# Reading the moving columns and writing the output columns of the main matmuls from last to first

## The chip, the cores and the metric

The kernel runs on one core of one Trainium2 chip. The metric is the device time of that core in microseconds (us). Three executions of the kernel before took 2253.87, 2256.15 and 2256.82 us; the median is 2256.15 us.

## The reference

One inference step of a two-layer decoder trunk (the constant DEPTH is 2) over a prompt of 256 tokens and 8 single-token samples, which share all weights. Everything is float32, D_MODEL is 2048.

```
for i in range(DEPTH):                                    # DEPTH = 2
    hp, hs = rmsnorm(xp, g_mix_pre[i]), rmsnorm(xs, g_mix_pre[i])
    if i % 2 == 0:   # w_in 2048 x 4608, window attention + gated width-3 convolution, w_out 2048 x 2048
        op, osm = even_prompt(hp, ...), even_sample(hs, ...)
    else:            # w_in 2048 x 4096, gelu, layernorm, 128 x 128 position mixing, w_out 2048 x 2048
        op, osm = cmlp_prompt(hp, ...), cmlp_sample(hs, ...)
    xp, xs = xp + rmsnorm(op, g_mix_post[i]), xs + rmsnorm(osm, g_mix_post[i])
    # ffn(h) = square(relu(h @ w_up)) @ w_down, hidden width 8192
    xp = xp + rmsnorm(ffn(rmsnorm(xp, g_ffn_pre[i]), w_ffn_up[i], w_ffn_down[i]), g_ffn_post[i])
    xs = xs + rmsnorm(ffn(rmsnorm(xs, g_ffn_pre[i]), w_ffn_up[i], w_ffn_down[i]), g_ffn_post[i])
```

It returns the two activations and the new windows and states of both groups. Nearly all arithmetic is in the dense products `h @ w`.

## The kernel before

The activations lie with channels on the 128 partitions and tokens in the free dimension: a tile such as `hhi` is 128 x 16 x 264, 16 channel tiles of 264 columns (T = 256 prompt tokens and 8 samples). The tokens of one channel tile are neighbours in memory, 4 bytes apart, so a product reads them in one run.

Every dense product goes in blocks of 256 output channels (BC). A block's weights are 2048 x 256 values. SyncE loads them in two halves of 1 MB into `raw` (four slots, so two blocks ahead). ScalarE writes their rounded high part `whi` (L586), VectorE the remainder `wlo` (L952), in quarters of four channel tiles. The activations are kept in the same manner as `hhi` and `hlo` (or `ahi` and `alo`). The high and the low parts have the type float32r.

TensorE's work on a block is `quarter` (L1342 and after), called four times. For each of the four channel tiles k of a quarter and each of the two output tiles j, three matmuls add into one PSUM region of 264 columns: `whi` with `hi` (L1353), `whi` with `lo` (L1354) and `wlo` with `hi` (L1355). So a block has 16 x 2 x 3 = 96 such matmuls. Each has its own weight load of 128 columns (called PEld in the profile) and streams 264 moving columns. These are the "main matmuls": 17088 of them in 178 blocks. The block number's parity picks one of two pairs of PSUM banks (0 and 1, or 2 and 3), and VectorE or another reader takes the finished pair out (for instance L1188, L1214) while the next block runs. Readers always wait for the whole block (`w_used`, raised by the last matmul of a quarter).

Beside them TensorE does small work in banks 4 to 7: transposes, attention, the position mixing (L1704), and the statistics of the norms. `statistic` (L1370, L1374) multiplies a constant 128 x 128 matrix with 264 columns of plain float32; `token_statistic` (L1381) multiplies with one column. Each plain float32 matmul stands in the trace as two.

The order on each engine is the order in which the code is written; waits on semaphores tie the engines together. Names that matter below: `ps` is PSUM, `out` is the PSUM region of a main matmul, `hi` and `lo` are its moving tiles, `L979` writes `hlo` after a norm.

Of the kernel before, what the change touches and what calls it, by code (L numbers as in the profile page):

```python
# [33 lines left out]
CH = D // P  # L34
# [3 lines left out]
T = SEQ + NB  # L38
# [46 lines left out]
def build(nc, io):  # L85
    ctx = ExitStack()
    with ctx:
        def sb(name, shape, dt=F32):
            return ctx.enter_context(nc.sbuf_tensor(name, shape, dt))
# [6 lines left out]
        whi = sb("whi", [P, CH, BC], F32R)  # L96
        wlo = sb("wlo", [P, CH, BC], F32R)
# [95 lines left out]
        ps = ctx.enter_context(nc.psum_tensor("ps", [P, 8, 512], F32))  # L193
# [1147 lines left out]
        def _(pe):  # L1341
            def quarter(n, par, q, hi, lo, operand=None):  # L1342

                if q == 0 and not (isinstance(n, int) and n < 2):
                    pe.wait_ge(taken, n - 1)
                pe.wait_ge(w_lo_ready, 4 * n + q + 1)
                for k in range(QK * q, QK * q + QK):
                    if operand:
                        operand(k)
                    for j in range(2):  # L1350
                        cols = slice(P * j, P * j + P)
                        out = ps[:, 2 * par + j, 0:T]
                        pe.matmul(out, whi[:, k, cols], hi[:, k, :], start=(k == 0), stop=False)  # L1353
                        pe.matmul(out, whi[:, k, cols], lo[:, k, :], start=False, stop=False)  # L1354
                        mm = pe.matmul(out, wlo[:, k, cols], hi[:, k, :], start=False, stop=(k == CH - 1))  # L1355
                mm.then_inc(w_used, 1)

            def h_operand(k_norm):
# [52 lines left out]
            for q in range(NQ):  # L1411
                if q == NQ - 1:

                    pe.wait_ge(state_in, 16)
                    pe.wait_ge(l_in, 16 * 3)
                    pe.wait_ge(x_ready, PAIRS)
                    n_small = 2 * CH + 3 * CONVT
                    pe.transpose(ps[:, 7, 0:n_small], g_rows[0:n_small, 1, :], ident[0:n_small, 0:n_small])
                    for c in range(CONVT):
                        mm = pe.transpose(ps[:, 4, 16 * c:16 * c + 16], state_tok[0:2 * NB, P * c:P * c + P],  # L1420
                                          ident[0:2 * NB, 0:2 * NB])
                    mm.then_inc(state_turned, 1)
                quarter(0, 0, q, hhi, hlo, h_operand(0))
                for c in {0: (5, 6), 1: (7,)}.get(q, ()):
                    turn_x(c)
# [126 lines left out]
            for n in range(1, N_EOUT):  # L1552
                for q in range(NQ):
                    quarter(n, n % 2, q, hhi, hlo)
                    even_task(n, q)
# [13 lines left out]
            def product(n0, hi, lo, operand, pairs=UNIT // 2):  # L1569
                with pe.Fori(0, pairs) as i:  # L1570
                    for par in range(2):
                        for q in range(NQ):
                            quarter(n0 + 2 * i + par, par, q, hi, lo, operand if par == 0 else None)
# [11 lines left out]
            for c in range(CONVT):  # L1585
                mm = pe.transpose(ps[0:2 + NB, 4 + c // 4, P * (c % 4):P * (c % 4) + P], z_last[:, c, :], ident[:, :])
# [178 lines left out]
```

## Time and profile before

| What | Before |
|---|---|
| three executions, us | 2253.87, 2256.15, 2256.82 |
| profiled execution: time, us | 2253.87 |
| its span, first to last instruction, us | 2253.9 |
| TensorE busy | 2204.5 us, 98% |
| VectorE busy | 1249.2 us, 55% |
| ScalarE busy | 996.3 us, 44% |
| GpSimd busy | 237.5 us, 11% |
| bytes moved by DMA | 386.72 MB, mean 172 GB/s |
| main matmuls | 17088 of 17771 matmuls in the trace |

How to read it: the profiled execution is the shortest of the three, and nothing lies around its span, so its time is its span. Matmuls overlap in the array. The duration of one (about 0.29 us) is therefore longer than the distance from one start to the next, and it is this distance, here called the pitch, that adds up to the span. A pitch is read either from the starts in the timeline or from a count of matmuls over a stretch in which TensorE has no gap.

### The profile page before, as it was taken

The page shows a single profiled execution, that of the slowest core. Times are in us where ns is not written, and L with a number is a line of the kernel's source. Part 1 is how long each engine was busy: PE and PEld are TensorE (multiplying, and loading weights), DVE is VectorE, ACT ScalarE, POOL GpSimd, SP SyncE. Part 2 cuts the span into 40 slices and gives each one's busy share as a digit, 9 for nine tenths or more (in the row PEclk, how much of TensorE's full clock was granted, in tenths as well). Part 3 has the DMA queues.
Part 4 walks back from the last instruction along what each step waited for, and adds up shares of the span by engine and source line. Part 5 has one row for each costly group of instructions (what it writes and reads, how often), then busy time and mean ns, then how long its engine had stood idle before and what let it go on. Part 6 is the DMA issues. An engine that isn't in the chain of part 4 may idle for free.

```text
span 2253.9 us, 43497 instructions
## 1 busy us (share of the span) xinstructions
PE 2204.5 (98%) x17771; PEld 2183.2 (97%) x17771; DVE 1249.2 (55%) x1318; ACT 996.3 (44%) x1243; POOL 237.5 (11%) x178
## 2 busy tenths in 40 slices
PE   7999998999999999999989999989999999999999
PEld 7999997999999999999979999989999999999998
DVE  7556756654554455455576675575445545545543
ACT  5544444443443344344444564444334434434443
POOL 3001213000000000011241201220000000001112
PEclk9999999999999999999999999989999999999999
DMA  6854453555655655555535455545555555555551
GB/s 215 229 172 133 155 178 112 187 178 176 186 171 184 212 179 182 173 185 169 185 112 185 155 168 181 172 130 170 185 175 178 182 173 184 172 182 179 174 177 68
DMA packets 380631, 386.72 MB, mean 172 GB/s; under 512 B 6805, under 2 KB 378317, under 8 KB 380431
## 3 DMA queue, kind: packets, MB, share of 16 engines
q1 hardware_dynamic: 374530, 380.02, 53.8%
q10 hardware_dynamic: 6036, 5.80, 0.8%
q8 instruction: 45, 0.74, 0.1%
q14 instruction: 20, 0.16, 0.0%
HBM read 380.10 MB, written 5.71 MB: 171 GB/s over the span
## 4 chain that ended last, share of the span: by engine, by line
PE 93%; DVE 5%; ACT 1%; DMA 0%; issue 0%; POOL 0%; DVEq 0%; SPq 0%; ACTq 0%
PE ps L1353 30%; PE ps L1354 30%; PE ps L1355 30%; DVE hlo L979 2%; DVE wlo L952 1%; DVE y L1001 1%; PE ps L1635 0%; PE ps L1704 0%; PE ps L1548 0%; DMA region<-in_x_prompt_dram 0%; PE ps L1534 0%; PE ps L1467 0%; DVE region L1336 0%; DVE y L1006 0%; DVE x L1007 0%; DVE rs_post L971 0%
## 5 line engine op out<-in xcount | busy, mean ns | idle before, releaser
L952 DVE TENSOR_TENSOR wlo<-raw,whi 128x1024 fp32r<-128x1024 f32 x712 | 894.5, 1259 | 823.1 <-ACT whi L586 822.8
L586 ACT ACTIVATE whi<-raw 128x1024 fp32r<-128x1024 f32 x712 | 753.1, 1060 | 1092.9 <-PE ps L1355 1088.7
L1353 PE MATMUL ps<-hhi,whi 128*128 128x264 f32 x3136 | 906.2, 289 | 32.8 <-DVE hlo L979 32.5
L1354 PE MATMUL ps<-hlo,whi 128*128 128x264 f32 x3136 | 900.1, 287 | 0.0
L1355 PE MATMUL ps<-hhi,wlo 128*128 128x264 f32 x3136 | 898.5, 287 | 0.0
L1354 PE MATMUL ps<-alo,whi 128*128 128x264 f32 x2560 | 730.4, 285 | 0.0
L1353 PE MATMUL ps<-ahi,whi 128*128 128x264 f32 x2560 | 729.3, 285 | 0.0
L1355 PE MATMUL ps<-ahi,wlo 128*128 128x264 f32 x2560 | 729.0, 285 | 0.0
L1353 PEld LDWEIGHTS ps<-hhi,whi 128*128 128x128 f32 x3136 | 598.5, 191 | 43.1 <-issue 29.5
L1355 PEld LDWEIGHTS ps<-hhi,wlo 128*128 128x128 f32 x3136 | 596.7, 190 | 0.0
L1354 PEld LDWEIGHTS ps<-hlo,whi 128*128 128x128 f32 x3136 | 596.6, 190 | 0.1
L1353 PEld LDWEIGHTS ps<-ahi,whi 128*128 128x128 f32 x2560 | 483.5, 189 | 0.4 <-issue 0.4
L1355 PEld LDWEIGHTS ps<-ahi,wlo 128*128 128x128 f32 x2560 | 482.1, 188 | 0.0
L1354 PEld LDWEIGHTS ps<-alo,whi 128*128 128x128 f32 x2560 | 481.5, 188 | 0.0
L464 POOL COPY acc_pre<-sq 128x528 f32<-128x528 f32 x5 | 4.3, 870 | 762.8 <-ACT sq L816 741.8
L1188 DVE TENSOR_TENSOR y<-y,ps 128x528 f32 (+2 forms) x66 | 45.2, 687 | 60.7 <-PE ps L1355 60.7
L467 POOL TENSOR_TENSOR acc_pre<-acc_pre,sq 128x528 f32<-128x528 f32 x35 | 56.8, 1623 | 156.7 <-ACT sq L816 140.5
L1214 DVE TENSOR_SCALAR region<-ps 128x528 f32<-128x528 f32 x64 | 45.2, 707 | 39.1 <-PE ps L1355 39.1
L467 POOL TENSOR_TENSOR acc_post<-acc_post,sq 128x528 f32<-128x528 f32 x24 | 41.4, 1725 | 224.2 <-ACT sq L606 224.2
L979 DVE SCALAR_TENSOR_TENSOR hlo<-x,gains,hhi 128x264 fp32r<-128x264 f32 x64 | 50.2, 824 | 1.0 <-ACT hhi L614 1.0
L614 ACT ACTIVATE hhi<-x,gains 128x264 fp32r<-128x264 f32 x64 | 29.5, 507 | 41.2 <-POOL x L490 26.2
L1217 DVE TENSOR_TENSOR alo<-region,ahi 128x528 f32 x64 | 45.3, 708 | 0.5 <-ACT ahi L822 0.5
(218 smaller groups left out, 763.2 us busy)
## 6 DMA issues: line engine op xcount, KB each, us to landing
raw<-in_w_ffn_up_dram SPq DMA_DIRECT2D x128, 1024.0 KB, 5.3
raw<-in_w_ffn_down_dram SPq DMA_DIRECT2D x128, 1024.0 KB, 5.5
raw<-in_w_in_even_dram SPq DMA_DIRECT2D x36, 1024.0 KB, 5.2
raw<-in_w_in_cmlp_dram SPq DMA_DIRECT2D x32, 1024.0 KB, 5.3
raw<-in_w_out_even_dram SPq DMA_DIRECT2D x16, 1024.0 KB, 5.5
raw<-in_w_out_cmlp_dram SPq DMA_DIRECT2D x16, 1024.0 KB, 5.5
region<-in_x_prompt_dram SPq DMA_DIRECT2D x4, 512.0 KB, 8.5
out_y_prompt_dram<-region SPq DMA_DIRECT2D x8, 256.0 KB
```

What stands on the lines that cost most here:

```text
L467: pool.tensor_tensor(acc[:, :, :], acc[:, :, :], sq[:, s % 2], ALU.add).then_inc(sq_used, 1)
L586: act.activation(whi[:, QK * q:QK * q + QK, :], raw[:, 2 * par + q // 2, k, :], ACT.Copy).then_inc(w_hi_ready, 1)
L614: ins = act.activation(hhi[:, t, :], x[:, t, :], ACT.Copy, scale=gains[:, G_PRE[k], t:t + 1])
L952: dve.tensor_tensor(wlo[:, QK * q:QK * q + QK, :], raw[:, 2 * par + q // 2, k, :], whi[:, QK * q:QK * q + QK, :].bitcast(F32), ALU.subtrac ...
L979: ins = dve.scalar_tensor_tensor(out=hlo[:, t, :], in0=x[:, t, :], scalar=gains[:, G_PRE[k], t:t + 1], in1=hhi[:, t, :].bitcast(F32), op0= ...
L1001: dve.tensor_tensor(y[:, 2 * c:2 * c + 2, :], y[:, 2 * c:2 * c + 2, :], twice(rs_post[:, :]), ALU.mult).then_inc(scaled, 1)
L1188: return dve.tensor_tensor(dst, dst, src, ALU.add) if add else dve.tensor_copy(dst, src)
L1214: dve.tensor_scalar(relu[:, :, :], pair(par), 0.0, None, ALU.max).then_inc(taken, 1)
L1217: dve.tensor_tensor(alo[:, bass.ds(4 * i + 2 * par, 2), :], asq[:, :, :], ahi[:, bass.ds(4 * i + 2 * par, 2), :].bitcast(F32), ALU.subtrac ...
L1353: pe.matmul(out, whi[:, k, cols], hi[:, k, :], start=(k == 0), stop=False)
L1354: pe.matmul(out, whi[:, k, cols], lo[:, k, :], start=False, stop=False)
L1355: mm = pe.matmul(out, wlo[:, k, cols], hi[:, k, :], start=False, stop=(k == CH - 1))
```

## The change

In `quarter` the slice of the moving operand and the slice of the output are both taken with a step of -1 along the 264 columns. Column 263 is read first and its result is written to column 263, and so on down to column 0. The value that lands in each PSUM column is the same sum as before. The weights are read as before; no other matmul, wait, tile or loop is touched. Each engine has the same instructions in the same order as before. In the built program the moving pattern of such a matmul goes from step 1, offset 0 to step -1, offset 263, and so does the output's.

```
-                        out = ps[:, 2 * par + j, 0:T]
-                        pe.matmul(out, whi[:, k, cols], hi[:, k, :], start=(k == 0), stop=False)
-                        pe.matmul(out, whi[:, k, cols], lo[:, k, :], start=False, stop=False)
-                        mm = pe.matmul(out, wlo[:, k, cols], hi[:, k, :], start=False, stop=(k == CH - 1))
+                        out = ps[:, 2 * par + j, 0:T][:, ::-1]
+                        pe.matmul(out, whi[:, k, cols], hi[:, k, ::-1], start=(k == 0), stop=False)
+                        pe.matmul(out, whi[:, k, cols], lo[:, k, ::-1], start=False, stop=False)
+                        mm = pe.matmul(out, wlo[:, k, cols], hi[:, k, ::-1], start=False, stop=(k == CH - 1))
```

## Rows read from the trace of the kernel before

**Rows 1.** The page, busy time of each engine: us, share of the span, instructions.
```profile
PE 2204.5 (98%) x17771; PEld 2183.2 (97%) x17771; DVE 1249.2 (55%) x1318; ACT 996.3 (44%) x1243; POOL 237.5 (11%) x178
```

**Rows 2.** The page, busy tenths in 40 slices, with the granted clock.
```profile
PE   7999998999999999999989999989999999999999
...
PEclk9999999999999999999999999989999999999999
```

**Rows 3.** The page, the chain that ended last: shares by engine.
```profile
PE 93%; DVE 5%; ACT 1%; DMA 0%; issue 0%; POOL 0%; DVEq 0%; SPq 0%; ACTq 0%
```

**Rows 4.** The page, the main matmuls: count, busy us, mean ns, idle before, releaser.
```profile
L1353 PE MATMUL ps<-hhi,whi 128*128 128x264 f32 x3136 | 906.2, 289 | 32.8 <-DVE hlo L979 32.5
L1354 PE MATMUL ps<-hlo,whi 128*128 128x264 f32 x3136 | 900.1, 287 | 0.0
L1355 PE MATMUL ps<-hhi,wlo 128*128 128x264 f32 x3136 | 898.5, 287 | 0.0
L1354 PE MATMUL ps<-alo,whi 128*128 128x264 f32 x2560 | 730.4, 285 | 0.0
L1353 PE MATMUL ps<-ahi,whi 128*128 128x264 f32 x2560 | 729.3, 285 | 0.0
L1355 PE MATMUL ps<-ahi,wlo 128*128 128x264 f32 x2560 | 729.0, 285 | 0.0
```

**Rows 5.** Windows: us, busy us and count of each engine, clock, DMA share, GB/s.
```profile
600.00:1000.00 400.00, 400.00 (x3267) 400.00 (x3266) 203.13 (x189) 165.70 (x177) 9.64 (x5) 1.00 0.59 184
1500.00:2100.00 600.00, 600.00 (x4900) 600.00 (x4900) 304.43 (x282) 248.28 (x264) 8.46 (x5) 1.00 0.57 178
386.56:388.70 2.14, 2.14 (x12) 2.14 (x11) 2.14 (x4) 0.58 (x3) 1.49 (x1) 0.50 0.00 0
```

**Rows 6.** Timeline of TensorE at 386 us: start us, us, engine, line, operation.
```profile
386.39 0.42 PE L1354 MATMUL ps<-hlo,whi 128*128 128x264 f32 x1
386.61 0.42 PE L1355 MATMUL ps<-hhi,wlo 128*128 128x264 f32 x1
386.83 0.42 PE L1353 MATMUL ps<-hhi,whi 128*128 128x264 f32 x1
```

**Rows 7.** Timeline of TensorE at 1184 us.
```profile
1184.01 0.28 PE L1354 MATMUL ps<-hlo,whi 128*128 128x264 f32 x1
1184.12 0.28 PE L1355 MATMUL ps<-hhi,wlo 128*128 128x264 f32 x1
1184.24 1.05 PE L1370 MATMUL ps<-acc_pre,mean_w 128*128 128x264 f32 x4
1185.16 0.39 PE L1353 MATMUL ps<-hhi,whi 128*128 128x264 f32 x1
```

**Rows 8.** Timeline of TensorE at 2137 us.
```profile
2137.44 1.39 PE L1381 MATMUL ps<-mean_w,acc_pre 128*128 128x1 f32 x12
2138.69 0.37 PE L1353 MATMUL ps<-ahi,whi 128*128 128x264 f32 x1
```

**Rows 9.** Groups of PE by line: a plain 264-column group, one column, 16 apart.
```profile
L1370 PE MATMUL ps<-acc_pre,mean_w 128*128 128x264 f32 x16 | 4.2, 386 | 0.0
...
L1381 PE MATMUL ps<-mean_w,acc_pre 128*128 128x1 f32 x12 | 1.4, 243 | 0.0
...
L1601 PE MATMUL ps<-region,mean_w 1*128 1x16 f32 x2 | 0.4, 268 | 0.0
```

**Rows 10.** Waits of PE: us in total, times, longest us.
```profile
PE ps L1353 <- DVE hlo L979: 32.5, 20, 8.0
```

## The prediction

> **What bounds the kernel.** I read the busy line first, then the slices, then the chain, then the groups of TensorE, and last the distance from start to start. TensorE is busy 98% of the span, VectorE 55%, ScalarE 44% [rows 1]. The slices show that this is no average over unlike stages: TensorE stands at 9 in nearly every slice, at full granted clock [rows 2]. The chain that ended last runs 93% over TensorE [rows 3]. Six groups hold the main matmuls, 3 x 3136 + 3 x 2560 = 17088, with no idle time before them but 32.8 us at L1353 [rows 4], nearly all of it waits for `hlo` after a norm [rows 10]. So what counts is the pitch of a main matmul.
>
> A duration of 285 to 289 ns [rows 4] is not the pitch, because matmuls overlap. Two long stretches in which TensorE has no gap give it: 400 us over 3267 is 122.4 ns, 600 us over 4900 is 122.4 ns [rows 5]. That is the same number in two different halves of the kernel, with VectorE and ScalarE at about half load in both. In all: 17088 x 122.45 = 2092 us of the 2253.9 us span. The other 162 us are small matmuls, the waits, the start and the end. The profiled execution's time is its span; the median of the three runs is 2.3 us above it.
>
> **The change, part by part.** No instruction, wait or DMA is added, removed or moved. The three matmuls of `quarter` keep 264 columns, the same bytes, the same bank and the same weight load. Two things differ in each of the 17088: the addresses on the moving side descend, and so do those on the PSUM side. So the sum has one line: 17088 x (new pitch - 122.45 ns). Each nanosecond of pitch is 17.1 us. Nothing hides it: with TensorE without a gap for hundreds of us, every extra nanosecond of pitch is on the path. Nor can another engine take a gain away soon, since VectorE is at 203 of 400 us there and the DMAs at 0.59 [rows 5].
>
> Nothing else follows from the order within a matmul. Readers of PSUM wait for a whole quarter, not for its first column, so it does not matter to them which column is written last. In three matmuls in a row that add into the same region each column comes up again one pitch later, before as after, because all three are turned. At the step from one region to the next (and from a small matmul to a main one) the order is free anyway. The waits of 32.5 us end with VectorE's `hlo` [rows 10], which the change does not touch.
>
> No row of this kernel has a descending run, so the two new costs have to be bounded. I take them together, since one pitch shows both.
>
> From above. At half clock the pitch of the same matmul is 220 ns [rows 6] (12 starts in 2.14 us at clock 0.50 [rows 5]), which is 264 columns at one per 1.2 GHz tick. At full clock the plain float32 matmul of the same 264 columns has a pitch of (1.05 us - 0.386 us) / 3 = 221 ns [rows 7, 9]. So if the array got only one column per 1.2 GHz tick from the descending run, or could write only one, the pitch would be 220 to 222 ns: 17088 x 99.5 = +1700 us. A middle value comes from the only row that reads columns far from each other, L1601 with 16 columns 512 bytes apart: 268 ns against 243 ns for one column [rows 9], 25 ns for 15 more columns, 1.7 ns each, where L1370 has 221 / 264 = 0.84 ns. That form is another (one row of the array, plain float32) and the two durations are of two and twelve records, so I hold it for weak; it says only that a price between nothing and double is possible.
>
> From below. The stream itself needs no more than half the pitch at half clock, 220 / 2 = 110 ns, and 122.4 are paid. If what fills these 12.4 ns had to do with ascending order, the pitch could fall to 110: 17088 x -12.4 = -212 us. A one-column matmul with the same weight load has a pitch of about (1.39 - 0.24) / 11 = 0.104 us [rows 8, 9], so the weight load alone costs nearly as much as the stream. The 12.4 ns may thus come from the weight side. In that case a descending stream that is up to 12 ns dearer would cost nothing either.
>
> The value that I take is zero. The two ends, -212 and +1700 us, lie far apart and the row nearest to the changed matmul is the matmul itself: same type, same count, same bytes, neighbours still neighbours, the run still in one piece and its even length still splitting into aligned pairs. The two rows at the upper end are nearest in what would have to happen, not in what is changed. Sum: 2253.9 + 0, and 2256 us against the median.
>
> The Trainium skill says on its page Advanced Engine Details and Errata, section Memory Cachelines, that SBUF delivers at full rate as long as a 16-byte line is hit at least twice in a row. A descending float32 run hits each line four times, so by this rule the moving side costs nothing; no row before can confirm it. The same section, and PSUM — Partial Sum Buffer in its Specifications table, speak against the change: PSUM lines have 8 bytes, "any non-contiguous AP slows matmuls significantly". The page does not say whether a step of -1 is contiguous. Taken strictly it makes the output side pay, and the sum would be the one with the upper end; taken by pairs in a line, 263 with 262, it costs nothing. VectorE's page of the microarchitecture (Vector Engine (DVE) Microarchitecture Reference, section 5.1) counts steps of +1 and of -1 alike for its paired modes; that is another engine, and I use it only to lean.
>
> **The rivals.**
> 1. The pair is lost: two neighbouring columns are served in one 1.2 GHz tick only when they ascend, on the moving or the output side. For: at full clock 264 columns go by in 122.4 ns, 1.8 per tick of 1.2 GHz, so whatever feeds the array and takes its results works at twice that tick or in pairs. Against: the pairs stay aligned. Pitch 222 ns, time 2254 - 2092 + 17088 x 0.222 = 3955 us. The stretches at half clock would not change, at 220 ns already. The strict reading of the skill's PSUM rule above is this case.
> 2. A partial price: a cost per line or per instruction of a descending run, from above 12 ns on if the weight side covers the first, otherwise from 0. The middle row's ratio, 1.7 / 0.84 = 2.0 put on 122.4 ns, would reach past the upper bound, so it sets no place between the ends. 5 ns are +85 us, 2341 us against the median; half way, 172 ns, is +847 us, 3103 us.
> 3. The other side, faster: the 12.4 ns above the stream come from the moving run and the weight run both ascending, and starting on the same side of their tiles, and a descending stream passes the weight reads with less waiting. From 110 ns: 2254 - 212 = 2042 us, between them in proportion, decided as soon as the pitch drops by 0.3 ns (5 us). For: the 12.4 ns are unexplained, and plain float32 pays for its 264 columns in two streams only 221 ns, 110.5 each. Against: the pitch is equal in stretches with unlike load and with different tiles, which looks like a fixed cost per matmul.
> 4. The change doesn't do what it says: since both sides are turned together, something between the code and the engine may turn both back. Its time is that of no change, 2256 us, and its chance is part of my forecast's; an experiment with one side alone would be needed to tell.
>
> **How the numbers follow.** No change in pitch (with 4): 0.59. Pair lost: 0.20. Partial price: 0.14. Faster: 0.07. 0.2% is 4.5 us, a pitch of 0.26 ns, and about what a measurement of this kernel can tell from nothing. So faster 0.07, same 0.59, slower 0.34. The likeliest case alone would be 2251 to 2261 us. It leaves 0.41 outside; the range therefore reaches over the partial price to the pair lost, 3955 us and a little for the start, and down to 2240 for a small gain. That leaves out 0.06.
>
> **What would show it.** Right: in the windows at 600 to 1000 and 1500 to 2100 us again 3267 and 4900 matmuls, durations of the six groups at 285 to 289 ns, steps of 0.12 us in the timeline, waits for `hlo` at 32.5 us, the statistic's pitch at 0.22. Rival 1: steps of 0.22 us at granted clock 1.00, about 1800 matmuls in 400 us, VectorE's share down to a third. Rival 2: a pitch between. Rival 3: more than 3267. My forecast is wrong if the pitch moves by 0.3 ns either way while the clock row stays as it is; if the pitch stands and the time moves, I have overlooked a wait.

## The result and the profile after

The changed kernel took 2229.61 us (median of 4 runs, 2228.98 to 2229.94), the kernel before 2255.86 us in the same comparison (4 runs). The ratio is 0.9885, with a 95% interval of 0.9873 to 0.9897: the change makes the kernel 1.15% faster, 26 us. The prediction had no change as likeliest, and the lower end of its range was 2240 us.

The page of the changed kernel, busy line, slices and chain:

```profile
PE 2176.4 (98%) x17771; PEld 2154.9 (97%) x17771; DVE 1249.9 (56%) x1318; ACT 995.6 (45%) x1243; POOL 236.9 (11%) x178
...
PE   7999998999999999999989999989999999999999
...
PEclk9999998999999999999999999989999999999999
...
PE 92%; DVE 6%; ACT 1%; DMA 0%; issue 0%; DVEq 0%; SPq 0%; ACTq 0%
```

TensorE is as full as before [rows 1 to 3], over a span of 2227.3 us, 26.6 us shorter. (The execution behind this trace took 2228.98 us, 1.7 us more than its span, and so it is in every later run. The span of 2253.9 us of the kernel before therefore belongs more likely to its execution of 2255.57 us than to the one of 2253.87 us; that its time is its span was a wrong reading, by under 2 us.) VectorE, ScalarE and GpSimd work as long as before, to within 1 us. Nothing has left the path; what stands on it has become shorter.

The groups of the main matmuls, after (columns as in rows 4), and the waits for `hlo` (as in rows 10):

```profile
L1353 PE MATMUL ps<-hhi,whi 128*128 128x264 f32 x3136 | 902.6, 288 | 33.4 <-DVE hlo L979 33.1
L1354 PE MATMUL ps<-hlo,whi 128*128 128x264 f32 x3136 | 895.4, 286 | 0.0
...
L1353 PE MATMUL ps<-ahi,whi 128*128 128x264 f32 x2560 | 727.0, 284 | 0.0
```

```profile
PE ps L1353 <- DVE hlo L979: 33.1, 20, 8.0
```

The durations fell by 1 to 2 ns, the waits stayed [rows 4, 10]. The end of a matmul is modelled in the trace, so the pitch is read from counts. Windows of the changed kernel, columns as in rows 5:

```profile
600.00:1000.00 400.00, 400.00 (x3313) 400.00 (x3312) 205.53 (x190) 168.18 (x180) 11.41 (x6) 1.00 0.59 186
1500.00:2100.00 600.00, 600.00 (x4968) 600.00 (x4967) 308.40 (x286) 252.00 (x268) 12.08 (x7) 1.00 0.58 181
```

3313 matmuls instead of 3267 in 400 us, 4968 instead of 4900 in 600 us [rows 5]: the pitch is 120.8 ns and was 122.4. Over all neighbouring main matmuls at full clock the mean distance of starts went from 122.44 to 120.88 ns (steps of 200 ns and more, which hold a wait, left out). The some 16,800 such steps make 26.3 us, nearly the whole of the 26.6 us. At half clock the step is 220 ns in both kernels.

Looking closer than a window gives the cause away. The starts in one block of the kernel before, the channel tile k = 3, and in the changed kernel, tiles k = 1 and k = 2 (start us, us, engine, line):

```profile
708.92 0.29 PE L1353 MATMUL ps<-ahi,whi 128*128 128x264 f32 x1
709.05 0.28 PE L1354 MATMUL ps<-alo,whi 128*128 128x264 f32 x1
709.17 0.29 PE L1355 MATMUL ps<-ahi,wlo 128*128 128x264 f32 x1
709.30 0.29 PE L1353 MATMUL ps<-ahi,whi 128*128 128x264 f32 x1
...
709.68 0.28 PE L1353 MATMUL ps<-ahi,whi 128*128 128x264 f32 x1
```

```profile
710.76 0.28 PE L1353 MATMUL ps<-ahi,whi 128*128 128x264 f32 x1
710.88 0.28 PE L1354 MATMUL ps<-alo,whi 128*128 128x264 f32 x1
711.00 0.28 PE L1355 MATMUL ps<-ahi,wlo 128*128 128x264 f32 x1
...
711.48 0.28 PE L1353 MATMUL ps<-ahi,whi 128*128 128x264 f32 x1
...
712.22 0.28 PE L1353 MATMUL ps<-ahi,whi 128*128 128x264 f32 x1
```

Six matmuls take 0.76 us at k = 3 before (709.68 - 708.92), 0.72 us at k = 1 after and 0.74 us at k = 2 after. The pitch is not one number, it hangs on the channel tile. Averaged over all blocks from 550 to 1040 us and from 1500 to 2130 us, by the matmul's place in its block (worked out from the starts in the two traces, ns):

```
k (same again for k + 8)      0      1      2      3      4      5      6      7   mean
before                     119.9  121.9  121.3  125.4  123.8  122.1  124.9  120.8  122.5
changed                    120.2  120.3  123.1  122.4  120.4  120.1  120.1  120.1  120.8
```

The pattern repeats after eight channel tiles, in both kernels, to 0.1 ns. Neighbouring moving tiles start 1056 bytes apart, and 8 x 1056 = 33 x 256. The weight tiles start 1024 = 4 x 256 bytes apart. So the place of the moving run against the weights' run comes back after eight tiles, in units of 256 bytes. Four of the eight tiles of the changed kernel (k = 0 and 5 to 7) stand at a flat 120.0 ns, with 0.8 ns more at the first of the six matmuls; only k = 2 and 3 are over 121 ns.

### The profile page after: what moved, and what is told of

The parts are those of the page before. It is cut to its first block, busy times and chain, and to the rows that moved or that the text cites. A ratio compares the mean times of both kernels' runs of the same rounds, so it can differ in the third digit from the quotient of the medians.

```text
span 2227.3 us, 43497 instructions
## 1 busy us (share of the span) xinstructions
PE 2176.4 (98%) x17771; PEld 2154.9 (97%) x17771; DVE 1249.9 (56%) x1318; ACT 995.6 (45%) x1243; POOL 236.9 (11%) x178
## 4 chain that ended last, share of the span: by engine, by line
PE 92%; DVE 6%; ACT 1%; DMA 0%; issue 0%; DVEq 0%; SPq 0%; ACTq 0%
PE ps L1353 30%; PE ps L1355 30%; PE ps L1354 30%; DVE hlo L979 2%; DVE wlo L952 1%; DVE y L1001 1%; ACT whi L586 0%; PE ps L1635 0%; DMA region<-in_x_prompt_dram 0%; PE ps L1704 0%; PE ps L1548 0%; PE ps L1534 0%; PE ps L1467 0%; DVE region L1336 0%; DVE y L1006 0%; DVE x L1007 0%
```

## The experiments

Theory A: TensorE reads the moving columns of one matmul while it loads the weights of the next. Both are reads of SBUF, they get in each other's way, and how often depends on where the two runs stand and which way they go. Theory B: the writing side does it. That loading and streaming go on at the same time is to be seen in the kernel before, where the weight load of each matmul (PEld) begins with the matmul ahead of it:

```profile
600.05 0.29 PE L1355 MATMUL ps<-hhi,wlo 128*128 128x264 f32 x1
600.05 0.20 PEld L1353 LDWEIGHTS ps<-hhi,whi 128*128 128x128 f32 x1
600.18 0.29 PE L1353 MATMUL ps<-hhi,whi 128*128 128x264 f32 x1
600.18 0.19 PEld L1354 LDWEIGHTS ps<-hlo,whi 128*128 128x128 f32 x1
```

All pitches below are means over the same two stretches as in the table, each from the one execution of a kernel that was traced; the times beside them are medians of all its executions. All times of the kernel before are medians from the same chip as the kernel they stand beside.

**One side at a time.**

```
 e1:  out = ps[:, 2 * par + j, 0:T]              pe.matmul(out, whi[:, k, cols], hi[:, k, ::-1], ...)   (lo the same)
 e2:  out = ps[:, 2 * par + j, 0:T][:, ::-1]     pe.matmul(out, whi[:, k, cols], hi[:, k, :], ...)      (lo the same)
```

> Only the moving columns are read from last to first; the output columns are written first to last (so the products' columns come out mirrored). Theory A (the 1.6 ns of pitch come from the reading side: moving read and weight read get in each other's way less when the moving run descends): pitch 120.8 ns as in the changed kernel, time about 2230 us, and the same pattern over the 48 matmuls of eight channel tiles. Theory B (it is the writing side, the order in which PSUM columns are written): pitch 122.5 ns, 2256 us. Theory C (both sides must be turned together, only their agreement matters): neither, at least as slow as before.

> Only the output columns are written from last to first; the moving columns are read first to last (columns come out mirrored). Theory A: pitch 122.5 ns, 2256 us, pattern as before the change. Theory B: 120.8 ns, 2230 us. Theory C: neither.

Moving side alone: 2229.22 us (4 runs), ratio 0.9886 (0.9869 to 0.9902), pitch 120.8 ns, and the same eight pitches as the changed kernel to 0.1 ns. Output side alone: 2256.25 us (10 runs), ratio 1.0002 (0.9992 to 1.0011), pitch 122.5 ns and the eight of the kernel before. Windows of e1 and of e2:

```profile
600.00:1000.00 400.00, 400.00 (x3312) 400.00 (x3312) 205.88 (x191) 167.97 (x181) 11.44 (x6) 1.00 0.60 186
```

```profile
600.00:1000.00 400.00, 400.00 (x3268) 400.00 (x3267) 203.15 (x189) 165.88 (x178) 9.63 (x5) 1.00 0.59 184
```

So the gain comes whole from reading in descending order. Writing PSUM in descending order costs and gives nothing. Theories B and C are out, and so is the fourth rival (that the change doesn't do what it says).

**Is it the tile that is read, or the place in the program?**

```
-  hi[:, k, :]                   lo[:, k, :]
+  hi[:, 4 * par + q, :]         lo[:, 4 * par + q, :]            (e3)
+  hi[:, 4 * par + q, ::-1]      lo[:, 4 * par + q, ::-1]         (e4, output turned too)
```

> Ascending as before the change, but all 24 matmuls of a quarter stream one channel tile, number 4 x parity + quarter, so tiles 0 to 7, instead of tile k (the products are other ones). The tiles start 1056 bytes apart, that is 32 bytes further each in units of 256 bytes. Theory A (what counts is where the moving tile starts against the weights' run): the pitch is constant within a quarter after its first matmuls and differs by tile, over a spread of about 4 to 6 ns between the best and the worst tile (by the means of the run before: tiles 0 and 7 about 120 to 121, tiles 3, 4 and 6 about 124 to 125). Theory D (the pattern over 48 matmuls comes from the place of the instructions in the program, not from the addresses): the pattern over k stays as before whatever tile is read.

> Turned, and one channel tile per quarter (number 4 x parity + quarter) as in the ascending one before. Theory A': the quarters on tiles 2 and 3 have pitches of 122 to 124 ns, the six others 120.0; mean about 120.6 to 120.9. Rival (descending reads simply cost less everywhere, and the tile change costs): all eight at 120.0.

```
tile                           0      1      2      3      4      5      6      7
e3, ascending                121.4  121.9  121.0  121.8  123.3  121.7  120.6  120.0
e4, turned                   120.0  120.0  124.4  122.2  120.0  120.0  120.0  120.0
```

(Means after the first channel tile of each quarter; e3 took 2243.44 us in one run, e4 2228.93.) With one tile read throughout a quarter the pattern over k goes and the pitch is the tile's own. Theory D falls. In e4 two tiles are dear, the same two as in the changed kernel, and six stand at 120.0 flat. The rival that descending reads are cheaper everywhere fails on tiles 2 and 3. In e3 the values by tile are not those I had expected: tiles 3, 6 and 4 were the dear ones in the kernel before, and of these only tile 4 is here. The pitch at a place depends on what went before it, so a number from one arrangement doesn't carry over to another.

**Is the weight load the other party?** First a case in which it reads almost nothing of SBUF: one weight column, 128 times over.

```
-  pe.matmul(out, whi[:, k, cols], ...)
+  pe.matmul(out, whi[:, k, P * j:P * j + 1].to_broadcast([P, P]), ...)       (wlo the same)
```

> Ascending as before the change, but the weight load reads one column 128 times over instead of 128 columns (all 128 output channels of a tile come out alike), so the weight side reads a single spot of SBUF while the moving side reads as before. Theory A (the two reads collide): the pattern over the eight tiles goes or becomes quite another one; if a fixed spot is hit seldom, the pitch is near the floor of 120 ns. Rival (the moving read alone has the pattern, or writes of other engines): pattern and 122.5 ns stay as before.

Windows of e7, with ascending reads:

```profile
600.00:1000.00 400.00, 400.00 (x3332) 400.00 (x3331) 207.82 (x193) 170.35 (x183) 11.35 (x6) 1.00 0.60 186
1500.00:2100.00 600.00, 600.00 (x4997) 600.00 (x4996) 311.03 (x288) 255.22 (x273) 13.96 (x8) 1.00 0.58 182
```

120.1 ns for every one of the eight tiles, 2219.03 us in one run. (Within a tile the single steps still go from 116.7 to 122.5 ns; their mean is what is flat. The weight load takes 189 ns in the trace, before 190, so it isn't a shorter load that shows here.) The moving reads and their order are those of the kernel before, and VectorE, ScalarE and the DMAs write as before. So the extra above 120 ns is not the moving read's own and not a matter of the other engines: it needs a weight load that walks over its 512 bytes.

**Tiles that all stand alike.** The weight tiles are put 1056 bytes apart, like the moving tiles, so the relation is the same for every k; e6 is turned as well.

```
-  whi = sb("whi", [P, CH, BC], F32R)         +  whi = sb("whi", [P, CH, T], F32R)       (wlo the same; L586 and L952 write 0:BC)
-  cos = sb("cos", [P, T])                    +  cos = y[:, CH - 1, :]                   (sin: y[:, CH - 2, :])
```

> Ascending as before the change; the channel tiles of both weight buffers are put 1056 instead of 1024 bytes apart (264 instead of 256 columns, 8 unused), the same distance as the moving tiles, so that weights and moving tile of every k stand to each other as those of k = 0 do. To make room the rotary tables lie in two tiles of y that are free then. Theory A with the place of the moving run against the weights' run as the cause: no pattern over k is left, the pitch is that of tile 0, about 120 ns, time about 2214 us (17088 x -2.45 ns). If only the absolute place of the moving run counts: pattern and 122.5 ns stay, 2256 us.

> The change as made (moving and output turned) and the channel tiles of both weight buffers 1056 instead of 1024 bytes apart, as in the experiment before. In the changed kernel the tiles k = 2, 3 (and 10, 11) cost 123.1 and 122.4 ns, all others 120.1 to 120.4. Theory A': the extra of tiles 2 and 3 comes from where the descending moving run stands against the weights' run; with all tiles standing as k = 0 does it is gone: pitch 120.1 ns, 0.7 ns less than the changed kernel, time about 2229.6 - 12 = 2217 us. Rival (the absolute place of the moving tile alone): tiles 2, 3 stay dear, 2229 us.

e5: 2245.45 us (4 runs), ratio 0.9955 (0.9938 to 0.9971), pitch 121.8 ns. The pattern over eight tiles is gone, as expected; in its place two values alternate, 122.1 for even tiles and 121.4 to 121.7 for odd ones. The level is not the 120 ns expected. e6: 2219.01 us (5 runs), ratio 0.9839 (0.9825 to 0.9853), pitch 120.14 ns at every tile. Tiles 2 and 3 have lost their extra, though their moving runs are read as before and lie only 1024 bytes (4 x 256) further on; the weights' place has changed. Windows of e6:

```profile
600.00:1000.00 400.00, 400.00 (x3332) 400.00 (x3331) 208.12 (x193) 170.61 (x184) 12.11 (x7) 1.00 0.60 187
1500.00:2100.00 600.00, 600.00 (x4996) 600.00 (x4996) 311.28 (x289) 254.92 (x272) 13.96 (x8) 1.00 0.58 182
```

and the starts of its tile k = 2, six matmuls in 708.23 - 707.51 = 0.72 us where the changed kernel had 0.74:

```profile
707.51 0.28 PE L1353 MATMUL ps<-ahi,whi 128*128 128x264 f32 x1
707.63 0.28 PE L1354 MATMUL ps<-alo,whi 128*128 128x264 f32 x1
707.75 0.28 PE L1355 MATMUL ps<-ahi,wlo 128*128 128x264 f32 x1
707.87 0.28 PE L1353 MATMUL ps<-ahi,whi 128*128 128x264 f32 x1
...
708.23 0.28 PE L1353 MATMUL ps<-ahi,whi 128*128 128x264 f32 x1
```

The counts are those of e7, where the weight load reads one spot: e6 pays nothing more for the two reads meeting than a kernel does whose weight load doesn't walk. It also beats the changed kernel, by 10.6 us.

**Direction or place?** In the layout of e5 and e6 all activation tiles are moved against the weights by padding.

```
+  pad = sb("pad", [P, 16 or 32 or 48])       # 64, 128 or 192 bytes
   x = sb("x", [P, CH, T])
```

> Ascending as before the change, weight tiles 1056 bytes apart, and 192 bytes of padding between the weight buffers and all activation tiles, so that every moving tile stands to its weights as channel tile 6 did in the experiment with one tile per quarter (120.0 ns there, as tile 7). Theory A' (place and direction together decide; there is nothing better in descending as such): pitch 120.1 ns, time about 2219 us, as good as the turned kernel with the same weight tiles. Rival (descending reads are better whatever the place): stays near 121.8 ns, 2245 us.

> Turned, weight tiles 1056 bytes apart, and 64 bytes of padding before the activation tiles, so that every moving tile stands to its weights as channel tile 2 does in the changed kernel (124.4 ns in the experiment with one tile per quarter). Theory A': pitch about 124.4 ns, 2219 + 17088 x 4.3 ns = 2292 us, slower than the kernel before the change although it is turned. Rival (descending is better whatever the place): 120.1 ns, 2219 us.

> Ascending, weight tiles 1056 bytes apart, and 128 bytes of padding, so that every moving tile stands to its weights as channel tile 4 did in the ascending experiment with one tile per quarter (123.3 ns). Theory A': pitch about 123.3 ns, 2219 + 17088 x 3.2 ns = 2274 us. Rival (the place of the activation tiles does not matter once the weight tiles are moved): 121.8 ns, 2245 us.

> Ascending, weight tiles 1056 bytes apart, 64 bytes of padding before the activation tiles. Measured so far in this layout: ascending 121.8 (0 bytes), 120.1 (128), 122.2 (192); turned 120.1 (0), 123.0 (64). Theory P (place and direction together; neither direction is better as such): somewhere from 120 to 124 ns, and over the four places the means of the two directions within 1 ns. Theory Q (descending is better as such, 64 bytes is a bad place for both): over 123.0 ns, above 2273 us.

> Turned, same layout, 128 bytes of padding. Theory P: anything from 120 to 124 ns, a floor of 120.1 no likelier than not. Theory Q: 120.1 ns, 2219 us, since ascending already is at the floor there.

> Turned, same layout, 192 bytes of padding. Theory P: anything from 120 to 124 ns. Theory Q: under the ascending 122.2 ns (2249 us).

```
bytes moved             0                  64                 128                192
ascending    121.8 ns 2245.45 us   120.8 ns 2228.28 us   120.1 ns 2220.02 us   122.2 ns 2249.16 us
turned       120.1 ns 2219.01 us   123.0 ns 2273.14 us   121.3 ns 2237.53 us   120.1 ns 2217.74 us
```

(e12 to e14 have two runs each, e10 and e11 four, e9 twelve.) Ratios to the kernel before: e9 0.9977 (0.9954 to 1.0001), e10 1.0077 (1.0063 to 1.0092), e11 0.984 (0.9826 to 0.9855), e12 0.9875 (0.9846 to 0.9903), e13 0.9916 (0.9887 to 0.9944), e14 0.9828 (0.9799 to 0.9857). Windows of e10, turned, and of e11, ascending:

```profile
600.00:1000.00 400.00, 400.00 (x3272) 400.00 (x3271) 203.72 (x189) 165.45 (x177) 9.57 (x5) 1.00 0.58 184
1500.00:2100.00 600.00, 600.00 (x4862) 600.00 (x4861) 301.75 (x280) 244.19 (x259) 6.60 (x4) 1.00 0.57 178
```

```profile
600.00:1000.00 400.00, 400.00 (x3332) 400.00 (x3331) 208.00 (x193) 169.87 (x183) 11.44 (x6) 1.00 0.59 186
1500.00:2100.00 600.00, 600.00 (x4997) 600.00 (x4996) 311.07 (x289) 254.75 (x272) 13.96 (x8) 1.00 0.58 182
```

A turned kernel can be slower than the kernel before (e10, by 0.8%), and an ascending one can stand at the floor (e11, level with the best turned ones). The mean over the four places is 121.2 ns ascending and 121.1 turned; of the times it is 2235.7 and 2236.9 us. Theory P holds for these four places, though it asked for little (anything from 120 to 124 ns): turning gains nothing as such, it is one of several ways to change how the two reads meet. Theory Q fails at 64 and at 128 bytes, where the turned kernel is the slower one. My values for single places were poor: e10 was slower as expected but by 17 us and not 36, e9 and e11 came out the wrong way round (2249 and 2220 us where 2219 and 2274 were expected). So the distance between the two runs matters, but it doesn't fix the pitch by itself: the distance of tile 4 costs 123.3 ns in e3 and 120.1 in e11, both ascending.

The traces show one reason why. e10 has a pitch of 400 / 3272 = 122.2 ns in the first stretch and 600 / 4862 = 123.4 in the second, with the same code. And e9 and e12:

```profile
600.00:1000.00 400.00, 400.00 (x3242) 400.00 (x3241) 201.93 (x187) 164.54 (x177) 9.62 (x5) 1.00 0.58 183
1500.00:2100.00 600.00, 600.00 (x4950) 600.00 (x4950) 307.28 (x285) 249.86 (x265) 8.46 (x5) 1.00 0.58 181
```

```profile
600.00:1000.00 400.00, 400.00 (x3332) 400.00 (x3331) 207.42 (x192) 170.66 (x183) 11.42 (x6) 1.00 0.60 187
1500.00:2100.00 600.00, 600.00 (x4951) 600.00 (x4950) 307.58 (x285) 251.94 (x268) 12.08 (x7) 1.00 0.57 180
```

123.4 ns in the first stretch of e9 and 121.2 in the second, 120.1 and 121.2 in e12. The starts tell more (worked out from the traces, means over blocks of 96). As long as main matmuls follow each other without a break, some 5300 of them in the longest stretches, the mean holds to 0.01 ns, over `hhi` and `ahi` alike. It changes only across a break: small matmuls, a wait, or a stretch at half clock.

```
stretch without a break, about, us    400 to 1040    1040 to 1130    1480 to 2120
e9, ascending, 192 bytes                 123.47          121.25          121.25
e10, turned, 64 bytes                    122.36          122.36          123.47
e12, ascending, 64 bytes                 120.14          120.14          121.25
e11 and e14                              120.14          120.14          120.14
e13, turned, 128 bytes                   121.25          121.25          121.25
```

So the two streams can fall into more than one rhythm with each other at the same place. The levels lie 1.11 ns apart, 6.7 ns for the six matmuls of a tile. A rhythm once taken up is kept until a break, and the next break can bring another. What at a break picks it is not shown; no run changes the breaks alone. The pitches 120.8, 122.2 and 123.0 ns of the table above are mixtures of two levels (e12 stands at the floor for over a third of its time), and the traced execution needn't be the median one: e10 took 2266.54 us there, and 2272 to 2274 in its three others. The twelve executions of e9 spread from 2242 to 2267 us, where the kernel before spreads over 3.4 us. In the two kernels of the change itself nothing of the kind is seen: 122.5 ns in every long stretch of the one, 120.8 in every one of the other.

**What is the floor?** Turned, with columns 0 to 7 left out for k = 1 to 15:

```
+  c0 = 8 if k else 0
+  out = ps[:, 2 * par + j, c0:T][:, ::-1]       hi[:, k, c0:T][:, ::-1]       lo[:, k, c0:T][:, ::-1]
```

> Turned, and the main matmuls of k = 1 to 15 leave out columns 0 to 7 (256 columns, the start at column 263 is kept; those of k = 0 have all 264). What sets the floor of 120 ns? If it is the moving stream with a fixed extra: 8 columns at 2.4 GHz are 3.3 ns, pitch 116.7 (and 117.5 with the dear tiles). If the weight load sets it: 120 stays.

2192.48 us in one run, mean pitch 118.5 ns, single tiles (after the first) from 117.5 to 119.7 and steps from 114 to 123 ns. Eight columns fewer brought 2.4 ns of the 3.3 that they take to stream. So the weight load alone doesn't set 120 ns; but the pitch is not clean enough to tell a fixed extra of 10 ns from one in proportion to the columns. What fills the time between 110 ns of stream and the floor of 120 stays open.

## Why the prediction was wrong

- The bound was read rightly: TensorE without a gap, everything on the pitch, 17.1 us per nanosecond. A pitch 1.6 ns shorter gave 26.3 of the span's 26.6 us; nothing hid it or gave it back. The stretches at half clock stayed at 220 ns.
- The step that failed is the one that set the new pitch equal to the old: "the value that I take is zero", because the row nearest to the changed matmul is the matmul itself. It came out at 120.8 ns against 122.4. The argument holds for the stream, which needs no less or more when turned. It leaves out that a third of the bytes read in each pitch are the weight load's (512 beside 1056), and that turning changes how the moving run meets them. The third rival (0.07) named the two parties, and the sign came out as it said. That was in part luck: by its mechanism a descending stream passes the weight reads with less waiting, and at the four places of e5, e6 and e9 to e14 the turned kernel is faster at two and slower at two. The places of this kernel's tiles happened to be on the good side. Its size was taken as all 12.4 ns above the stream; of these only 2.4 ns are collisions (122.5 against 120.1 in e7 and e6), and the turned kernel wins 1.6 of them. The other 10 ns no experiment but the narrower one touched. One of its reasons, plain float32 in two streams of 110.5 ns each, is not in the rows: they show one record every 221 ns, and two such records for a matmul.
- The argument against it was an average read as a constant. I held the equal pitch of two long windows [rows 5] for a sign of a fixed cost per matmul. A window of 400 us holds 34 blocks and so every place of the moving tiles equally often; it must come out the same. The starts within one block, 0.12 to 0.13 us apart, differ by tile in the trace of before as well; the eight means from 119.9 to 125.4 ns were there to be worked out.
- The first and second rival, 0.34 together, were carried by the output side and by the price of a descending line. Measured: the output side 0.3 us of 2256 (e2, inside its interval), the moving side no cost at all at tiles 0, 1 and 4 to 7 (e4 at 120.0 ns). The case of 3955 us was far out, and the range was wide on the wrong side and ended 10 us too high on the other.
- On the PSUM rule: the Trainium skill says in Advanced Engine Details and Errata, section Memory Cachelines, that any non-contiguous pattern in PSUM slows matmuls. A step of -1 is not such a case here: 2256.25 against 2255.94 us. The rule of the Trainium skill on 16-byte lines of SBUF in the same section, under which a descending float32 run costs nothing, agrees with e4's 120.0 ns; it says nothing of two reads at a time. That the direction matters at a given place is shown here (e5 against e6); which way the weight load walks is not, nor what in SBUF or TensorE makes one read wait for the other. The page TensorE: Matmul & The Clock Gate of the Trainium skill, section Weight-path perf modes, mentions reversed weights for one mode that this kernel doesn't use; no run here can turn the weights to show it.

## What to carry to other kernels

When matmuls follow each other without a gap and each has its own weight load, work out the distance of starts by the matmul's place in its loop, not only over long windows: a pattern that repeats with the addresses of the operands is a cost that layout can remove. Giving weight tiles and moving tiles the same distance in memory, and then trying two or three offsets between them, was worth 1.6% here (2219 against 2256 us), more than turning the reads in the old layout (1.15%). Test a change of order together with the place, since each alone can go either way, and look at each long stretch by itself and at several executions: the same kernel can run at more than one level.

## What was not expected of the hardware

- The moving read of a matmul and a weight load beside it cost each other up to 5.4 ns of 120 by channel tile (k = 3 of the kernel before, 125.4 ns; single steps there go from 116 ns to 131.6 at k = 6), by their places, with a period of 256 bytes; with a weight load from one spot the pitch is 120.1 ns whatever the tile.
- The first of the six matmuls of each tile takes 0.8 ns more than the floor in e6, and in e4 where a quarter on a new tile begins (at five of the six flat tiles); within a tile's quarter in e4 it doesn't.
- The same program can run at two pitches in two stretches (121.25 and 123.47 ns in e9), each held to 0.01 ns over thousands of matmuls until a break, and its runs spread over 1.1% at a granted clock of 0.988 to 0.991.
- Descending order of the output columns in PSUM is free at full rate: ratio 1.0002.
